# A trunk of two hybrid layers on one core: a new table of places in attention, and experts' outputs scattered into token rows

## What is computed

```
u = rmsnorm(h); proj = u @ w_in
o_a = hgrn2(...)                 # gated linear recurrence, 4 heads of 128, chunkwise
o_b = diff_attn(...)             # (softmax(q1 k1) - lambda softmax(q2 k2)) v, rotary, 4 heads of 64
o_c = fox_attn(...)              # softmax(q k + D_t - D_s) v, D = cumulated log forget, 4 heads of 64
h = h + concat(o_a, o_b, o_c) @ w_out
u = rmsnorm(h)
# 4 groups of 8 experts: best group, then the best 2 experts in it; gates from both softmaxes
for each token and each of its 2 experts e:  y = (silu(u @ w1[e]) * (u @ w3[e])) @ w2[e]
h = h + sum over the 2 experts of gate * y
```

## Time and profile before

| | us |
|---|---|
| median of the runs (3) | 3391.37 |
| lowest and highest run | 3385.06, 3393.1 |
| the profiled execution | 3382.7 |
| its span, first to last instruction | 3380.4 |

### The profile page before, as it was taken

The page is one execution under the profiler, slowest core; times in us unless marked ns, Lnnn a source line. Parts: engine busy times, 40 slices in busy tenths (PEclk is TensorE's granted clock), DMA queues, the critical chain, the costliest instruction groups (busy, mean ns, idle before and its releaser), DMA issues.

```text
span 3380.4 us, 44938 instructions
## 1 busy us (share of the span) xinstructions
PE 3049.2 (90%) x16960; PEld 1982.5 (59%) x16960; DVE 1525.9 (45%) x2625; ACT 828.4 (25%) x1917; POOL 169.0 (5%) x239
## 2 busy tenths in 40 slices
PE   8999988898895999999699999888989769999995
PEld 5666556676543555555376665666764345555553
DVE  5666535655325222323366663465553342222325
ACT  4333234432110111111143331344221101111113
POOL 1300000000000000000200000000000000000002
PEclk9999999898996999999899999998989979999996
DMA  5820100001015999999810000000010079999996
GB/s 179 254 58 13 46 13 7 8 16 54 18 44 215 410 409 412 409 410 406 307 56 26 26 26 27 7 13 2 19 51 29 32 303 412 414 418 415 410 411 229
DMA packets 136560, 592.74 MB, mean 175 GB/s; under 512 B 13000, under 2 KB 47816, under 8 KB 119016
## 3 DMA queue, kind: packets, MB, share of 16 engines
q1 hardware_dynamic: 105688, 491.42, 36.9%
q0 software_dynamic: 20400, 72.69, 6.4%
q10 hardware_dynamic: 10336, 26.75, 2.1%
HBM read 524.56 MB, written 66.26 MB: 175 GB/s over the span
## 4 chain that ended last, share of the span: by engine, by line
PE 72%; DVE 15%; ACT 4%; DMA 4%; issue 3%; POOL 1%; SPq 0%; POOLq 0%; PEld 0%; PEldq 0%; ACTq 0%; DVEq 0%
PE ps L1557 7%; PE ps L1563 7%; PE ps L1479 7%; PE ps L1598 6%; PE ps L1125 6%; PE ps L1588 6%; PE ps L1188 6%; PE ps L1615 3%; PE ps L1429 3%; PE ps L1282 3%; PE ps L1243 2%; PE ps L1269 2%; DVE negmax L1866 2%; DMA arena<-w 2%; PE ps L1351 2%
## 5 line engine op out<-in xcount | busy, mean ns | idle before, releaser
L1188 PE MATMUL ps<-arena 128*128 128x260 f32 x1024 | 286.5, 412 | 3.6 <-DVE arena L1799 2.1
L1557 PE MATMUL ps<-arena 128*128 128x512 f32 x544 | 245.8, 605 | 3.2 <-DVE arena L2357 2.0
L1866 DVE TENSOR_REDUCE negmax<-ps 16x1 f32<-16x16 f32 (+8 forms) x216 | 151.2, 704 | 213.6 <-PE ps L1248 211.9
L817 ACT ACTIVATE arena<-ps,negmax 16x16 f32<-16x16 f32 (+8 forms) x216 | 150.8, 698 | 386.0 <-DVE negmax L1866 385.6
L1598 PE MATMUL ps<-arena 128*64 128x256 f32 x2176 | 242.3, 381 | 0.0
L1563 PE MATMUL ps<-arena 128*128 128x256 f32 x1088 | 240.4, 379 | 0.0
L1351 PE MATMUL ps<-arena 128*128 128x256 f32 x1024 | 229.6, 382 | 11.7 <-ACT arena L910 11.7
L1588 PE MATMUL ps<-arena 128*128 128x512 f32 x544 | 239.1, 592 | 0.0
L1563 PEld LDWEIGHTS ps<-arena 128*128 128x128 f32 x1088 | 206.7, 190 | 42.6 <-issue 16.3
L1479 PE MATMUL ps<-arena 128*128 128x512 f32 x512 | 222.4, 592 | 0.0
L1351 PEld LDWEIGHTS ps<-arena 128*128 128x128 f32 x1024 | 191.9, 190 | 46.9 <-ACT arena L910 21.3
(11 more groups left out here) (348 smaller groups left out, 4189.5 us busy)
## 6 DMA issues: line engine op xcount, KB each, us to landing
arena<-w SPq DMA_DIRECT2D x204, 2048.0 KB, 18.6
xg<-arena POOLq DMA_DIRECT2D x51, 512.0 KB, 12.4
xg<-arena ACTq DMA_DIRECT2D x34, 512.0 KB
arena<-w_in SPq DMA_DIRECT2D x16, 1024.0 KB, 6.5
xg<-arena ACTq DMA_DIRECT2D x68, 128.0 KB, 8.9
arena<-w_in SPq DMA_DIRECT2D x16, 512.0 KB, 4.0
arena<-w_out SPq DMA_DIRECT2D x2, 4096.0 KB, 14.0
u_rows<-arena SPq DMA_DIRECT2D x16, 512.0 KB, 2.6
```

The costliest lines, as they stand in the source:

```text
L1188: mm = pe.matmul(out, w_qk[b][:, k, :], uT[:, k, lo:hi], start=(k == 0), stop=(k == KD - 1), skip_group_check=True)
L1557: mm = pe.matmul(ps[:, 0, :], XT[:, c, :], W1[0][:, c, :], start=(c == 0), stop=(c == KD - 1))
L1866: v.tensor_reduce(negmax[0:r, at:at + 1], flat[0:r, side:side + wide_], AX.X, ALU.max, negate=True)\
```

## The change

It has three parts.

1. The two tables of places are new. The pieces are the same, their places and some banks differ. For forgetting heads the copy of the *second* bundle (tiles 4 to 8) moves from VectorE (L1892) to ScalarE; the first and the third bundle stay on VectorE.
2. Experts' outputs go to `y_rows`, which has two rows a token (first and second expert, next to each other). GpSimd writes them there by an indirect DMA (`write`), one for the large block (128 rows of 4 KB) and one for the small block (128 half rows of 2 KB). ScalarE's stores and `xg` with its zero fill are gone. `yb` may be written again when `m_free` has been raised, which GpSimd does when both writes of a round have landed. The small block is fetched one round ahead. Routing makes numbers of destination rows beside the token numbers; an empty slot gets a number out of bounds, and neither its fetch nor its write moves anything. This takes five VectorE instructions more a layer.
3. The rows are read back by nine plain loads on SP, one a tile, with a semaphore each. The next layer's forget weights are loaded behind tile 3, its other first weights behind tile 8.

```diff
@@ -154,25 +154,25 @@
 SLOTS_OF = 6
 
 PLAN_DA = {
...
-    4: [["e2@6"], ["a3.2@2"], ["f2@6"], ["a3.3@2"], [], ["b3@6"]],
-    5: [["a0.0@2+"], ["o@6"], [], ["c3@6"], ["a0.1@2+"], ["d3@6"]],
-    6: [[], ["e3@6", "a0.2@2+"], [], ["f3@6"], ["a0.3@2+"], ["h@6"]],
...
+    4: [["a0.0@2+", "e2@6"], [], [], [], ["b3@6", "f2@6"], ["a0.1@2+"]],
+    5: [["a0.2@2+"], ["a0.3@2+", "o@6"], [], ["c3@6"], [], []],
+    6: [["d3@6"], ["e3@2"], [], ["f3@6"], [], ["h@6"]],
...
@@ -852,6 +882,7 @@
                     late = new[1:] if n < HEADS and j == T - 2 else []
                     mine = 1 <= t <= TILES and (t - 1) // T < HEADS
                     parts_ = len(bundles((t - 1) % T)) if mine else 0
+                    middle = HEADS <= (t - 1) // T < ALL and len(bundles((t - 1) % T)) > 1
                     if new:
                         exps(new[0])
                     pieces_act(layer, slot)
@@ -865,7 +896,7 @@
                         for u in new[1:]:
                             exps(u)
                     pieces_act(layer, slot + 3)
-                    if parts_ > 1:
+                    if parts_ > 1 or middle:
                         turned(t - 1, 1)
...
+                        act.wait_ge(m_free, ONE + t)
                         act.activation(yb[:, 0, 0:512], ps[:, 3, :], ACT.Copy).then_inc(m_ya, 1)
-                        act.wait_ge(m_ya, ONE + t * 2 + 1)
-                        act.wait_ge(m_yv, ONE + t + 1)
-                        act.dma_start(xg[bass.ds(i * SPAN, P), :], yb[:, 0, :]).then_inc(m_out[0], 16)
 
                         act.wait_ge(m_h, ONE + t * 4 + 3)
                         act.wait_ge(m_g, ONE + t * 3 + 2)
@@ -1074,15 +1102,8 @@
                         act.activation(GT[:, 0:2, :].rearrange("p k n -> p (k n)"), ps[:, 7, 0:2 * P],
                                        ACT.Copy).then_inc(m_gtc, 1)
                         act.wait_ge(m_y[1], ONE + t + 1)
-                        act.wait_ge(m_out[1], 16 + t * 32)
...
@@ -1630,15 +1651,8 @@
                 pool.sem_inc(semaphore, ONE)
 
             pool.sem_inc(c_h, T)
-            for semaphore in m_out:
-                pool.sem_inc(semaphore, 16)
-
             wait_alone(pool, s_zero, 2)
 
-            wait_alone(pool, h_q, ONE + 1)
-            for b in range(SLOTS // P):
-                pool.dma_start(xg[b * P:(b + 1) * P, :].rearrange("p (a n) -> p a n", n=P),
-                               zeros.unsqueeze(1).to_broadcast([P, D // P, P])).then_inc(s_zfill, 16)
             for layer in range(depth):
...
+                        out_, last, from_ = ((y_rows, 2 * L - 1, yb[:, 0, :]), (y_halves, 4 * L - 1, yb[:, 1, 0:512]))[k]
+                        pool.tensor_copy(pick_to[:, k:k + 1], rows_to[k][:, bass.ds(i, 1)]).then_inc(m_pick, 1)
+                        wait_alone(pool, m_pick, ONE + nth)
+                        pool.indirect_dma_start(
+                            out=out_, out_offset=bass.IndirectOffsetOnAxis(ap=pick_to[:, k:k + 1], axis=0), in_=from_,
+                            in_offset=None, bounds_check=last, oob_is_err=False).then_inc(m_out[k], 16)
+
+                    turns, picks = before * 3 + 2 * layer, before * 4 + 3 * layer
                     wait_alone(pool, r_u, (layer + 1) * 16 * T)
                     fetch(0, 0, picks + 1)
+                    fetch(1, 0, picks + 2)
                     wait_alone(pool, m_xt, ONE + turns + 2)
-                    fetch(0, 1, picks + 2)
+                    fetch(0, 1, picks + 3)
                     with pool.Fori(0, count) as i:
                         t = before + i
-                        turns, picks = t * 3 + 2 * layer + 2, t * 2 + 2 * layer + 2
-                        wait_alone(pool, m_xt, ONE + turns - 2)
-                        fetch(1, i, picks + 1)
+                        turns, picks = t * 3 + 2 * layer + 2, t * 4 + 3 * layer + 3
+                        wait_alone(pool, m_xt, ONE + turns + 1)
+                        fetch(1, i + 1, picks + 1)
+                        wait_alone(pool, m_ya, ONE + t * 2 + 1)
+                        wait_alone(pool, m_yv, ONE + t + 1)
+                        write(0, i, picks + 2)
                         wait_alone(pool, m_xt, ONE + turns + 3)
-                        fetch(0, i + 2, picks + 2)
+                        fetch(0, i + 2, picks + 3)
+                        wait_alone(pool, m_ya, ONE + t * 2 + 2)
+                        write(1, i, picks + 4)
+                        for k in range(2):
+                            wait_alone(pool, m_out[k], t * 16 + 16)
+                        pool.sem_inc(m_free, 1)
                     wait_alone(pool, m_x[0], (before + count) * 16 + layer * 32 + 32)
+                    wait_alone(pool, m_x[1], (before + count) * 16 + layer * 16 + 16)
                     meet(pool, layer, 6)
-                if stop > 7:
-                    for j in range(T):
-
-                        if j == T - 1:
-                            wait_alone(pool, c_h, ONE + T + layer * T + 1)
-                        for k in range(2):
-                            pool.indirect_dma_start(
-                                out=ya[0:rows(j), j % (T - 1), k, :], out_offset=None, in_=xg[:, :],
-                                in_offset=bass.IndirectOffsetOnAxis(ap=dest[0:rows(j), k, j:j + 1], axis=0))\
-                                .then_inc(c_y[j // 2], 16)
 
...
+                    row_of(rows_to[0], id_parts[:, 2, :])
+                    v.tensor_scalar(ids[0], rows_to[0], 1, None, ALU.arith_shift_right).then_inc(r_ids, 1)
                     for k in range(2):
                         joined(id_parts[0:SMALL, k, :], ps[k * SMALL:(k + 1) * SMALL, 6, 2 * k * N_TURN:2 * (k + 1) * N_TURN])
-                    v.tensor_tensor(ids[1][0:SMALL], id_parts[0:SMALL, 0, :], id_parts[0:SMALL, 1, :], ALU.add)\
-                     .then_inc(r_ids, 1)
+                    for half in range(2):
+                        do(v.tensor_tensor(id_parts[half * SMALL:(half + 1) * SMALL, 2, :], id_parts[0:SMALL, 0, :],
+                                           id_parts[0:SMALL, 1, :], ALU.add))
+                    row_of(rows_to[1], id_parts[:, 2, :])
+                    do(v.tensor_scalar(ids[1], rows_to[1], 1, None, ALU.arith_shift_right))
+                    v.tensor_scalar(rows_to[1], id_parts[:, 2, :], -2.0, half_no, ALU.mult, ALU.add).then_inc(r_ids, 1)
                     v.wait_ge(r_ids, ONE + layer * 2 + 2)
                     rs.end()
```

The loads on SP, cut to the new lines:

```diff
+                if stop > 7:
+                    def load_outputs(j):
+
+                        r, first = rows(j), cols(j).start
+                        sp.dma_start(ya[0:r, j % (T - 1), :, :],
+                                     y_rows[2 * first:2 * (first + r), :].rearrange("(p k) d -> p k d", k=2))\
+                          .then_inc(c_y[j], 16)
+
+                    for j in range(T - 1):
+                        load_outputs(j)
+                        if j == 3 and layer + 1 < depth:
+                            load_forget(layer + 1)
+                    wait_alone(sp, c_h, ONE + T + layer * T + 1)
+                    load_outputs(T - 1)
+                    if layer + 1 < depth:
+                        load_recurrence(layer + 1)
             if stop >= PHASES:
                 for j in range(1, T):
```

90 lines of the change are left out of this document (48 added, 42 removed).

## The result

| | before | changed |
|---|---|---|
| median, us | 3388.22 (4 runs) | 3296.12 (4 runs) |
| lowest and highest | 3381.89, 3393.1 | 3293.22, 3298.38 |
| span of the profiled execution | 3380.4 | 3292.6 |

What follows compares the result with a forecast made beforehand. TensorE's idle and low-clock stretches were taken as the bound. Terms -34 (attention), -1.3, -0.7, +2.5, -9.7 and -6.4 made -49.6, rounded to -49: 3382.7 to 3333.7, or 3342.4 us on the median's side, range 3316 to 3380.

Steps and rivals of the forecast that it cites:

- The table's waits: Attention: new places for pieces remove TensorE's waits, 4.5 us a head over three heads, 13.5 us a layer.
- The waits of `e3` and `b`: Attention, pieces put between a head's tiles: 2.0 us a head gone at the first, net 0.5 at the second.
- `c3` against `o`: Attention: a piece waiting for VectorE to read `o` from bank 6; 1.4 of its 1.71 us taken as gained.
- late next: Attention, tile 7: the second turning would then wait for ScalarE's copy, some 0.7 us a head.
- nearly all and the clock with it: Rival, attention: the table gives nearly all and TensorE's clock rises, 25 to 30 us a layer, 3321 us; chance 0.15.
- Copy of second bundles: Attention, forgetting heads: moving the copy to ScalarE gains 1 us a head for four heads, bounds -1 and 3.
- Scatters in the loop: Expert loop: writes land 14 us into the round, 17 at worst, before `m_free` is wanted at 22.2; cost 0.
- the rival of a late scatter: Expert loop: writes land too late for `m_free`, 3430 us; chance 0.06, shared with costly new waits in attention.
- Rounds that waited for weights: Expert loop, late in layer 0: skipped empty slots end TensorE's waits for weights, -1.3 us, bounds -2 and 0.
- First round: First round of experts: the small block's fetch no longer waits for the second large one, -0.7 us.
- Routing: Routing: five more small VectorE operations in a chain, +1.25 us a layer, +2.5 in all.
- Behind the loop: Behind the expert loop: plain loads let VectorE start combining earlier, -9.7 us in layer 0 and -6.4 in layer 1.

Runs made afterwards that it cites:

- e2_tables: The kernel before with both new tables of places alone, VectorE still copying the second bundle: 3302.19 us, ratio 0.9746.
- e7_fill_before: The kernel before with unread matmuls ahead of waiting pieces and turnings in all heads, which spoiled sums and changed the experts chosen: 3393.16 us, ratio 1.001.
- e6_no_drain: The changed kernel without GpSimd's drain at the one meeting behind the expert loop: 3285.03 us, ratio 0.968.
- e9_keep_clock: The changed kernel with unread matmuls, 15 behind attention's last fold, 12 before the first fetched rows and 2 before their copy: 3291.64 us, ratio 0.9709.
- e10_both: The changed kernel with both e6_no_drain's removed drain and e9_keep_clock's unread matmuls: 3277.19 us, ratio 0.9678.
- e4: The changed kernel with the old tables and VectorE's copy, so scatters and plain loads alone: 3385.28 us, ratio 0.9997.
- e1: The kernel before with both new tables and ScalarE's copy of second bundles, stores and gathers as before: 3302.68 us, ratio 0.9755.
- e3: The kernel before with ScalarE's copy of second bundles alone, old tables: 3378.32 us, ratio 0.9974.
- e5: The kernel before with only the new table for differential heads: 3339.13 us, ratio 0.9845.
- e11_late_fill: The kernel before with 37 unread matmuls a layer, only at waits of the last two heads, in a bank without unfinished sums: 3374.35 us, ratio 0.9973.
- e8: The changed kernel with unread matmuls before its waits in all heads, which spoiled sums and changed the experts chosen: 3319.26 us, ratio 0.9785.

## Why the prediction was wrong, point by point

1. **The base and the place of the gain**: right. Time came from TensorE's waits and low-clock stretches in attention, and nothing from cheaper stores in the loop.
2. **The table's waits**: right in sum, wrong in parts. The forecast was 17 us of idle time a layer (bounds 2 to 30); the two traces show 18.4 and 19.5, e2_tables without the copy 19.7 and 19.3. The waits of `e3` and `b` went almost wholly. `c3` against `o` did not: in head 2 it grew from 1.71 to 2.95 us, where I had taken 1.4 off. The "late next" at the second turnings, 0.7 us a head, is there in part: the turnings' waits for ScalarE rose from 5.0 to 6.4 us a layer, and those for VectorE fell from 11.6 to 9.4, so that the sum hides it (16.8 to 16.0).

```profile
586.58 0.39 PE L1227 MATMUL ps<-rounded,gamma_r 128*128 128x260 f32 x1 [2.95 <-DVE arena L1819]
```

3. **The failed step**: the sum counted idle time only. It valued TensorE's busy time in attention at nothing, though the earlier trace rows showed 0.91 and 0.83 and the stage as a whole had 92 us a layer at the low clock. Those went down to 34 and 44, and the same matmuls took 26.2 and 21.2 us less a layer. This 47 us is nearly the whole miss of 51. The Trainium skill, "TensorE: Matmul & The Clock Gate", section "Terms", prices time at the low clock at half its length; the trace agrees roughly, with 26.2 us for 58 in layer 0 (0.45) and 21.2 for 48 in layer 1 (0.44). By that sentence alone the stage's 92 us had some 46 us a layer to offer beside the waits; the two heads of the earlier trace rows hold some 31 of the 92. I had it as a rival ("nearly all and the clock with it") at 0.15 and priced it too low: 25 to 30 us a layer in all, where 40 to 45 came. The argument by which I held it down was that head 2 took no longer than head 1 at a lower clock, so the late tiles were set by a chain of waits. e7_fill_before shows the flaw: with nothing made to wait less and the clock kept up, head 2 took 54.5 us, not 60. The clock was on its path. Part of the size is luck all the same: e6_no_drain, e9_keep_clock and e10_both, with the same code in this stage up to its last fold, spent 27 to 51 us a layer at the low clock in it.
4. **Copy of second bundles**: size right (8 us forecast, 8 measured alone), mechanism wrong. I said a wait of 0.6 us a head goes; the forgetting heads lost about 1 us of idle time a layer in all, the stage none, and the low time fell. Together with the tables nothing of it is left that can be measured, so the two terms should not have been added.
5. **Scatters in the loop**: right. Rounds are 34.5 us, TensorE doesn't wait for `m_free`, and the rival of a late scatter was far off. The landing was overestimated: median 8.0 us, most 10.0, where 14.7 had been taken from the fetches.

```profile
L1688 POOL DMA_INDIRECT y_rows<-arena x68: 999/1024/1037, 1050.1 to 3242.5; - x68
...
DMA to landing us min/median/max: 2.2/8.0/10.0
```

   Beside it stood a rule of the Trainium skill, "SBUF — State Buffer", section "Who interferes with whom". It gave no cost here: the issue took 0.999 to 1.037 us in all 68 writes, so no run here shows GpSimd held up by VectorE in the loop.
6. **Rounds that waited for weights**: right in sign, but within the spread. The 16 rounds took 552.0 us in both layers of the changed kernel and 552.0 to 555.1 in the other traces with scatters (e4, e6, e9, e10); with the old stores they took 552.2 to 557.4 (before, e1, e2, e3, e5, e11). Three microseconds of late weights come and go in either, and 0.7 us of the -2.5 in the table belongs to the next point.
7. **First round**: wrong sign. The 0.72 us did go, but the low clock behind the routing lasted longer: it ended about 6.0 us after the first turning before, and 8.6 us after it now. That costs 1.3 us in layer 0 (18.3 to 19.6); e9_keep_clock, which keeps TensorE busy there, takes 15.9.
8. **Routing**: right, +2.2 for +2.5.
9. **Behind the loop**: the term that failed is the meeting. I took 0.8 us from the landing to SyncE; it is 7.0, of which 5.9 are GpSimd's drain. The drain had stood in the trace of before with 3.01 us, unseen, since I read the meeting by who passed it and not by the chain into it. The load took 3.0 us from issue to combine instead of 2.4. In layer 0 another 1.2 us went behind the first combine (44.3 to 45.5 us from there to the next layer's heads), 0.5 of it a wait for tile 4's load, which stands behind the next layer's weights. Without the drain the distance is 8.0 us where 9.3 had been forecast, so the rest of the term held in sum (the scatter landed 2 us sooner than I took, the load 0.6 later). The estimate of 4.4 us for a 1 MB load had the second tile 0.3 us late; its combine stands at 1629.04 with no wait. And a slip: 1663.9 + 2.4 is 1666.3, so my own numbers give -9.9 and not -9.7.

## What to carry to other kernels

When TensorE's clock is below 1.00 in a stage, price a removed wait twice: once as idle time, and once as the low-clock time that follows it. Here each microsecond of idle time taken away brought more than one further microsecond of shorter matmuls. Where a wait can't be removed, a few matmuls that nobody reads, shorter in sum than the wait, can keep the clock (e9_keep_clock) or bring it back sooner (e11_late_fill); count them wait by wait, because a filler that outlasts its wait costs at once. A single trace of a low-clock stretch is one draw: look at the same code in a second one. And of a meeting of engines read the chain into it, the arriving instruction of each engine included: an engine that has just issued DMAs may take microseconds to drain.

## What the runs showed that I had not expected

- GpSimd's drain took 5.9 us behind a round of scatters and fetches and 3.0 us behind fetches alone (and 13.1 us in the kernel before behind the zero fill of `xg`, beside the recurrent heads); its shortest in the same kernel was 0.034 us. Other engines' drains had medians of 0.02 to 1.3 us.

```profile
L594 SPq DRAIN  x12: 7/58/70, 23.2 to 3206.8; - x12
L594 POOLq DRAIN  x12: 34/34/5922, 47.4 to 3246.0; - x12
```

- Adding work made a kernel faster: 37 idle-time matmuls a layer took 10 us off (e11_late_fill).
- The attention stage of one and the same code took 421.6 to 425.4 us in two kernels' traces at the same idle time (60.3 to 60.6), with 92 to 99 us at the low clock. So part of the spread between runs is the clock.
- The clock fell after waits of at most 1.07 us each, 3.3 us in sum (the rows of head 6 above), not after a long pause, and still fell there with 1.7 us of them left.
- Fillers that started a sum of their own in columns 384 to 512 of a bank went with wrong results where a sum in columns 0 to 260 of the same bank was unfinished (e7 and e8); in a bank that held none they did no harm (e11). The Trainium skill, "PSUM — Partial Sum Buffer", section "The four PSUM rules", has the reason: the first matmul of a sum clears the marks of the whole bank, so that the next one of the older sum overwrites instead of adding. The runs agree with it, but none tried it by itself.
